# One core, a two-layer hybrid decode step: when the paged cache of the sample tokens is read and used

## The reference, cut to what matters

```python
def latent_attend(q_lat, q_pe, c_kv, k_pe, mask):
    s = (jnp.einsum('bqhl,bkl->bhqk', q_lat, c_kv)
         + jnp.einsum('bqhr,bkr->bhqk', q_pe, k_pe)).astype(jnp.float32) * ATTN_SCALE
    ...
    p = jax.nn.softmax(s, axis=-1).astype(c_kv.dtype)
    return jnp.einsum('bhqk,bkl->bqhl', p, c_kv)
...
def gather_past(j):
    ckv = cache_ckv[page_table, j].reshape(n_seq, -1, KV_LORA)
    kpe = cache_kpe[page_table, j].reshape(n_seq, -1, QK_ROPE_DIM)
```

## Time and profile before

| | us |
|---|---|
| median of 3 runs | 910.09 |
| lowest and highest | 907.43, 912.4 |
| the profiled execution | 914.86 |
| its span (first to last instruction) | 913.2 |
| PE busy in the span | 785.9 (86%) |
| DVE busy | 319.0 (35%) |
| ACT busy | 206.4 (23%) |
| mean of what memory moved | 295 GB/s |

### The profile page before, as it was taken

One profiled execution on the slowest core, in us unless ns is written; L12 is line 12 of the kernel. 1 busy time (PEld: TensorE's weight loads), 2 busy tenths in 40 slices (PEclk: granted clock), 3 DMA queues, 4 the chain that ended last, 5 costly groups with the idle time before them and its releaser, 6 DMA issues.

```text
span 913.2 us, 16409 instructions
## 1 busy us (share of the span) xinstructions
PE 785.9 (86%) x6398; PEld 561.3 (61%) x6398; DVE 319.0 (35%) x948; ACT 206.4 (23%) x492; POOL 58.9 (6%) x101
## 2 busy tenths in 40 slices
PE   5999999799889776889899877999998799697894
PEld 5876667666556554558676554678665466364583
DVE  1433333333313212225346464126133133221435
ACT  2100234321111101022226352015321011110322
POOL 2401000000000000000051700000000000000000
PEclk9999999799999989979999988898999899988898
DMA  9853894389999999983166470896699999999601
GB/s 374 324 170 89 275 402 148 146 334 414 417 415 418 414 417 415 412 337 139 47 216 223 127 281 1 354 417 242 231 394 415 418 414 417 416 416 416 243 1 48
DMA packets 59376, 269.35 MB, mean 295 GB/s; under 512 B 7312, under 2 KB 12384, under 8 KB 38176
## 3 DMA queue, kind: packets, MB, share of 16 engines
q1 hardware_dynamic: 53072, 259.22, 71.7%
q10 hardware_dynamic: 3472, 5.13, 1.8%
q0 software_dynamic: 2752, 3.91, 1.5%
HBM read 261.05 MB, written 2.52 MB: 289 GB/s over the span
## 4 chain that ended last, share of the span: by engine, by line
PE 60%; DMA 27%; SPq 5%; DVE 3%; issue 2%; ACT 2%; ACTq 0%; DVEq 0%
PE bank L572 25%; DMA ring<-in_moe_w_up 19%; PE bank L703 10%; PE bank L682 5%; DMA xn_sq<-in_moe_w_up 5%; SPq L2036 4%; PE bank L744 3%; PE bank L729 3%; PE bank L597 2%; PE bank L971 1%; SPq L2028 1%; PE bank L824 1%; PE bank L534 1%; PE bank L829 1%; PE bank L517 1%
## 5 line engine op out<-in xcount | busy, mean ns | idle before, releaser
L703 PE MATMUL bank<-ring,arena 128*32 128x256 f32 x1344 | 116.4, 406 | 21.9 <-DMA arena<-in_moe_w_up 13.5
L572 PE MATMUL bank<-xn_sq,ring 128*128 128x264 f32 x480 | 110.2, 392 | 9.1 <-DMA ring<-in_stream 9.1
L572 PE MATMUL bank<-arena,ring 128*128 128x264 f32 (+1 forms) x456 | 110.3, 397 | 3.0 <-DVE arena L1482 2.2
L572 PEld LDWEIGHTS bank<-xn_sq,ring 128*128 128x128 f32 x480 | 92.5, 193 | 26.0 <-issue 9.9
L682 PEld LDWEIGHTS bank<-arena 128*128 128x128 f32 x864 | 100.5, 196 | 11.3 <-issue 10.4
L682 PE MATMUL bank<-arena 128*128 128x128 f32 (+1 forms) x864 | 103.7, 281 | 4.3 <-DMA ring<-in_moe_w_down 3.8
L1314 DVE TENSOR_TENSOR arena<-arena,bank 128x128 f32<-128x128 f32 x34 | 9.8, 287 | 267.8 <-ACT arena L1735 267.8
L572 PEld LDWEIGHTS bank<-arena,ring 128*128 128x128 f32 x456 | 87.0, 195 | 24.5 <-issue 8.5
L703 PEld LDWEIGHTS bank<-ring,arena 128*32 128x32 f32 x1344 | 65.0, 117 | 60.1 <-issue 41.2
L744 PE MATMUL bank<-arena 128*128 128x264 f32 (+1 forms) x288 | 73.0, 409 | 5.2 <-ACT arena L1751 5.2
L703 PE MATMUL bank<-xn_sq,arena 128*32 128x256 f32 x384 | 56.9, 463 | 17.2 <-DMA ring<-in_moe_w_up 17.2
(11 more groups left out here) (253 smaller groups left out, 835.1 us busy)
## 6 DMA issues: line engine op xcount, KB each, us to landing
ring<-in_moe_w_gate SPq DMA_DIRECT2D x38, 1024.0 KB, 21.7
ring<-in_moe_w_up SPq DMA_DIRECT2D x38, 1024.0 KB, 21.9
ring<-in_moe_w_down SPq DMA_DIRECT2D x38, 1024.0 KB, 22.8
ring<-in_stream SPq DMA_DIRECT2D x35, 1024.0 KB, 9.3
arena<-in_moe_w_down SPq DMA_DIRECT2D x26, 1024.0 KB, 21.0
arena<-in_moe_w_gate SPq DMA_DIRECT2D x14, 1024.0 KB, 19.7
arena<-in_moe_w_up SPq DMA_DIRECT2D x14, 1024.0 KB, 21.6
xn_sq<-in_moe_w_gate SPq DMA_DIRECT2D x12, 1024.0 KB, 21.6
```

Source lines behind the costliest of these rows:

```text
L572: t = mm(ps[:, 0:cols], lhs(k), rhs(k), start=(k == 0), stop=(k == n - 1))
L703: t = mm(bank[2 + r][p0:p0 + U, 0:F].rearrange("p (c f) -> p c f", c=2), x, w[i][:, :, k * F + c * P:k * F + (c + 1) * P], start=(k == 0), ...
```

## The change

The second group's four stages move from the head steps 12, 14, 16, 18 to 9, 11, 14, 16; DVE's last stage of it moves into its loop with them. The pages of samples 5, 6 and 7 are no longer loaded whole. Their key halves (columns 256 to 511) are issued once `("ss", 0, 1)` is full, their row halves (columns 0 to 255) once `("sv", 0)` is full, each with 8 transfers of 128 KB a sample, and the row halves have semaphores of their own, on which `sample_values(1)` waits. Sample 4 is still loaded whole, right behind sample 3. The 32 page numbers of samples 4 to 7 are read between the pages of sample 1 and those of sample 2. Line numbers of the changed kernel are 1 to 14 higher from there on.

```diff
@@ -75,7 +75,7 @@
 UW = 288
 SW = (TQ - 1) * NQ + TP
 PAIRS = KD // 2
-SAMPLE_AT = [[1, 3, 5, 7], [12, 14, 16, 18]]
+SAMPLE_AT = [[1, 3, 5, 7], [9, 11, 14, 16]]
 HK = DN + DR
 
 
@@ -405,6 +405,7 @@
         s_qps = sem("mla_qpe_samples")
         s_ng, s_pe, s_pn = (sem("att_" + n) for n in ("max", "exp", "p"))
         s_ckin = [sem(f"cache{i}") for i in range(TS)]
+        s_rowin = [sem(f"cache_rows{i}") for i in range(SB + 1, TS)]
         s_keys = sem("key_rope_rows")
         s_kpin = sem("cache_kpe")
         s_qz = sem("queries_padded")
@@ -987,6 +988,9 @@
                 for hf in range(2):
                     freed(pe, ("sp", B, hf))
                 freed(pe, ("sn", B))
+                if B:
+                    for x in s_rowin:
+                        pe.wait_ge(x, 16 * PAGES)
                 ps = open_bank(pe, ("sv", B))
                 for g in range(PAGES):
                     for i in range(SB):
@@ -1620,7 +1624,6 @@
             for c in range(KD):
                 if (H + 1 - 5) // 2 < c:
                     head_out(c)
-            sample_latent(1)
             ps = arrive(dve, "so")
             v.tensor_copy(oT[:, :, TP:T], ps[:, 0:KD * TS].rearrange("p (c b) -> p c b", c=KD))\
              .then_inc(is_free("so"), 1)
@@ -2020,13 +2023,18 @@
 
             def load_cache(b, pg):
 
-                if b > SB:
-                    arrive(sp, ("sv", b // SB - 1))
-                elif 2 <= b < SB:
+                if 2 <= b < SB:
                     arrive(sp, ("qn", KD - 1))
                 for n in range(PAGES):
                     sp.dma_start(CKX[b][n // 4][:, n % 4, :], a["cache_ckv"][bass.ds(pg[n], 1)].rearrange("o p f -> p (o f)"))\
                         .then_inc(s_ckin[b], 16)
+
+            def load_half(b, pg, at, done):
+
+                for n in range(PAGES):
+                    sp.dma_start(CKX[b][n // 4][:, n % 4, at:at + KL],
+                                 a["cache_ckv"][bass.ds(pg[n], 1), :, at:at + KL].rearrange("o p f -> p (o f)"))\
+                        .then_inc(done, 16)
 
             def load_expert(l, e, c, number):
 
@@ -2076,11 +2084,17 @@
                 fill(g)
             arrive(sp, "kpe")
             arrive(sp, "kv")
-            for B in range(TS // SB):
-                for i in range(SB):
-                    load_cache(SB * B + i, numbers[i])
-                if B == 0:
-                    numbers = [page_numbers(SB + i) for i in range(SB)]
+            load_cache(0, numbers[0])
+            load_cache(1, numbers[1])
+            numbers = numbers[2:4] + [page_numbers(SB + i) for i in range(SB)]
+            for b in range(2, SB + 1):
+                load_cache(b, numbers[b - 2])
+            arrive(sp, ("ss", 0, 1))
+            for b in range(SB + 1, TS):
+                load_half(b, numbers[b - 2], KL, s_ckin[b])
+            arrive(sp, ("sv", 0))
+            for b in range(SB + 1, TS):
+                load_half(b, numbers[b - 2], 0, s_rowin[b - SB - 1])
             for g in (G_WO, G_WO + 1, G_WO + 3, G_PIN1):
                 fill(g)
             expert_stream(1)
```

## The result

| | before | changed |
|---|---|---|
| median of 22 runs each, us | 908.9 | 914.38 |
| lowest and highest, us | 905.45, 914.14 | 909.92, 918.43 |
| the profiled execution, us | 914.86 | 914.19 |
| its span, us | 913.2 | 912.4 |

The ratio, changed to before, is 1.0041 with a 95% interval of 1.0023 to 1.0059. That is 3.7 us slower (2.1 to 5.4); the two medians lie 5.5 us apart. So the kernel became slower, clear of the noise and close to the 0.5% bound of the forecast (4.55 us): the middle of the interval lies under it, its upper end and the difference of the medians over it. The median of 914.38 is inside the forecast range of 905.5 to 916.5. The forecast shift was +0.8 us.

A forecast was written before the change was run, and what follows sets the result against it. Matmul lines and expert weights fill most of the chain, so only `wo`'s start counts: 8.4 us paid at the first group, 8 earned at the second, +0.8 us put on 910.09 gives 910.9, rounded to 911; range 905.5 to 916.5.

The forecast's parts named there:

- 0.5% bound of the forecast: Whole kernel's time: a change of under about 0.5% (4.55 us) can't be told from none.
- The old wait: Ahead of the second group's scores: PE's 4.0 us wait for a page transfer, forecast to go with 1.8 us of low clock.
- Rival A: SP's hole before sample 2: the 32 reads are hidden, at 0.36 us each; 8.4 us gained, 902.5 us; chance 0.08.
- Rival B: Ahead of group 0's scores: sample 4's transfers delay sample 3's landing by up to 5.2 us; 916.1 us; chance 0.12.
- Rival C: Second group's scores at step 9: they wait for key halves or rotary keys after all; say 913 us; chance 0.05.
- +0.3: At `so`: forecast 576.0 against 575.74 before, a shift carried unchanged through `wo` to the end.
- ends of the range: Second group up to `so`: alternative term values, among them sum 5.5 for 4.2 (+1.3) and wait for weights +0.9 us.
- The carrying over: Behind `wo`: any shift of its start reaches the kernel's end unchanged.
- the prediction's own sign: Behind `wo`: a stretch of another length than 334 us would show that carrying the shift to the end was wrong.
- Part 3: Second group three head steps earlier: last head scored behind the sum, exposed; 8.2 us from sum's end to `so`.

The follow-up runs named there:

- kernel with halves at steps 12 to 18: Changed kernel with 16 of the 32 page-number reads moved behind sample 4's issue and the second group back at head steps 12, 14, 16, 18: 903.46 us, ratio 0.9938.
- split-reads kernel: Changed kernel with 16 page-number reads (samples 4 and 5) left ahead of sample 2 and 16 (samples 6 and 7) behind sample 4's issue: 904.81 us, ratio 0.9947.
- reads-back kernel: Changed kernel with the 32 page-number reads of samples 4 to 7 put back behind sample 3's pages, all else kept: 903.83 us, ratio 0.9933.
- reads-only: Kernel before with only the 32 page-number reads moved ahead of sample 2; whole pages and head steps 12, 14, 16, 18 kept: 920.54 us, ratio 1.0118.
- run with the sum at step 16: The split-reads kernel with the second group's stages at head steps 9, 11, 16, 18 instead of 9, 11, 14, 16: 903.85 us, ratio 0.9930.

## Why the prediction was right, and where it was off

The mechanism held in its parts: the reads don't fit and delay the first group, the second group no longer waits for pages. The balance of the two did not come out as forecast. The change was to pay 8.4 us at the first group and earn about 8 at the second; it paid 9.55 and earned 5.2. The old wait and the low clock behind it were priced at 5.8 of the 8, so the three earlier head steps, which were to give the rest, gave nothing in this profile. That agrees with the kernel with halves at steps 12 to 18, which is as good without them. By the steps of the forecast:

| step | forecast | measured |
|---|---|---|
| first transfer of sample 2 | 493.9 | 492.80 |
| issue to landing, last of sample 3 | 6.4 | 6.99 |
| group 0's scores start | 508.8 | 508.75 |
| their duration | 7.28 | 8.45 |
| group 1's scores start, no wait | 542.2 | 543.55 |
| scores to weights | 12.3 | 11.9 |
| weights to sum | 9.1 | 10.25 |
| the sum | 4.2 | 5.9 |
| sum's end to `so` | 8.2 | 7.9 |
| `so` to `wo` | 3.1 | 3.7 |
| `wo` starts | 579.2 | 583.23 |

- **The reads.** 32 took 17.6 us, 0.55 us each. They don't fit in 11.5 us. Rival A's condition was not met, but its price came near: with the reads out of the way the kernel gained some 10 us against a forecast 8.4. The floor of about 600 ns that the Trainium skill ("DMA: Bandwidth & Descriptors", "Latency and other measured facts") gives for a `tensor_load` does not hold for these reads: the load took 0.26 us and the whole read 0.55.
- **The start of group 0** came out to 0.1 us by luck: SP was 1.1 us earlier than forecast, the 16 transfers took 0.4 us longer to issue (492.80 to 501.41) and the last one 0.6 us longer to land.
- **Rival B** fell: in the split-reads kernel sample 4 stands right behind sample 3, and group 0 waits for DVE only. The landing took 0.6 us more in the changed kernel than before, far from the 3.7 us that would have decided for B.
- **Rival C** fell: there was no wait for halves or rotary keys at step 9.
- **What was mis-sized is the low clock.** All that is missing between +0.3 and +4.35 us at `wo` stands in four terms: the scores of group 0 (+1.2), weights to sum (+1.15), the sum (+1.7) and `so` to `wo` (+0.6), less 0.5 from the others. In each the granted clock was 0.50 for a part of the stretch (five-us means of 0.53 to 0.66 above). The reads-back kernel, whose second group ran at the upper level here, has the forecast's own values for two of them: 8.8 us from weights to sum and 4.2 us for the sum. I had priced the first with the second group's 7.28 us, behind a gap of 4.0 us; behind 8.7 us it was 8.45. The length of the gap does not set this price alone: behind 12.1 us the same scores took 6.90, behind 9.1 us 8.28, behind 6.9 us 7.04. For the sum I took full clock although the row beside it (5.5 us) stood in the trace. Two of the four, the wait for weights and the sum, I had named as ends of the range and called the likelier, and then put only 0.5 us of them into the forecast.
- **The carrying over** of a shift at `wo` to the end held for the times: +4.35 us at `wo`, +3.7 by the ratio and +5.5 by the medians. By the prediction's own sign (334 us behind `wo`) it failed in the profiles: the stretch was 329.2 us instead of 334.3. In the reads-only and reads-back kernels it was 916.6 - 589.9 = 326.7 and 898.6 - 571.3 = 327.3. The 334.3 of the profile before contained the 5 us of low clock near the end.
- **Part 3** was right that the last head is exposed (8.2 forecast, 7.9 measured), and the run with the sum at step 16 shows that this is a trade of some 5 us against two head steps.

## What to carry to other kernels

A wait of an in-order queue is a hole of a certain length: count what is moved into it, per instruction and from a row, before moving it, and move only as much as fits. Here 16 reads of 0.55 us fit in 11.5 us and gained 0.5% with the halves, and 32 did not and lost 0.4%. When a gap on TensorE gets longer, price the matmuls behind it at the lower clock, from several rows if there are any: the same scores took 6.9 to 8.5 us behind gaps of 4 to 12 us, and 5.5 without. Do the same behind each later short wait.

## What was not expected of the hardware

- Eight extra single-column matmuls at 500 us brought a stop of 2.05 us on TensorE at 854.6, with no semaphore behind it, and lower clock behind that. All four kernels with additional PE instructions had a stop of 2.0 to 3.1 us between 851 and 857, and in all four it came behind the 6225th matmul, whatever had been added ahead. The ten profiles of kernels without them (that of before included) had none there. All 14 have one of 2.3 to 2.9 us behind the 2985th. So what a few instructions cost can depend on which later group of matmuls such a place comes to lie in.
- Two executions of nearly the same program can differ by 5 us at one place near the end by the granted clock alone (0.50 from 860 to 870 against 1.00).
